# Two halves of the PE array for the decay projections: odd token tiles on rows 64 to 96, even ones on rows 0 to 32

## The reference, cut to what matters

```
k, v, lr_f, lr_b = jnp.split(p_state, STATE_SPLITS, axis=-1)
logg_f = jax.nn.log_sigmoid((lr_f @ w_dec_f + b_dec_f).astype(jnp.float32)) / GLA_TAU
logg_b = jax.nn.log_sigmoid((lr_b @ w_dec_b + b_dec_b).astype(jnp.float32)) / GLA_TAU
```

## Time and profile before

| | us |
|---|---|
| median of 3 runs | 1681.29 (1680.9 to 1683.6) |
| the profiled execution's own time | 1684.84 |
| its span, first to last instruction | 1683.0 |
| PE busy in the span | 1601.7 (95%) |
| weight loads (PEld) busy | 1353.5 (80%) |
| DVE, ACT, POOL busy | 737.2 (44%), 574.1 (34%), 605.9 (36%) |
| mean granted clock of PE | 0.981 of full |

### The profile page before, as it was taken

The page is one execution under the profiler, slowest core; times in us unless marked ns, Lnnn a source line. Parts: engine busy times, 40 slices in busy tenths (PEclk is TensorE's granted clock), DMA queues, the critical chain, the costliest instruction groups (busy, mean ns, idle before and its releaser), DMA issues.

```text
span 1683.0 us, 23322 instructions
## 1 busy us (share of the span) xinstructions
PE 1601.7 (95%) x9320; PEld 1353.5 (80%) x9320; DVE 737.2 (44%) x1207; ACT 574.1 (34%) x924; POOL 605.9 (36%) x317
## 2 busy tenths in 40 slices
PE   5999999999899999999999899999989999999997
PEld 2777887877689989998999567888886888888887
DVE  2610225836565515662366384035755321221137
ACT  3634212523643313441143155442533422222231
POOL 1422111225333623563255343332242443444441
PEclk9899999989999999999999899999999999999999
DMA  9443332135412212212222572121062222222221
GB/s 372 156 159 136 108 130 89 39 128 187 186 63 76 78 48 76 76 63 66 72 76 94 228 260 83 63 76 51 26 238 101 77 98 100 90 98 100 88 90 60
DMA packets 50210, 185.25 MB, mean 110 GB/s; under 512 B 5254, under 2 KB 10246, under 8 KB 43208
## 3 DMA queue, kind: packets, MB, share of 16 engines
q1 hardware_dynamic: 44028, 170.29, 28.6%
q10 hardware_dynamic: 6092, 13.70, 2.2%
HBM read 172.44 MB, written 11.53 MB: 109 GB/s over the span
## 4 chain that ended last, share of the span: by engine, by line
PE 82%; DVE 6%; issue 4%; ACT 3%; POOL 2%; DMA 1%; SPq 1%; ACTq 0%; DVEq 0%; POOLq 0%
PE A L975 57%; PE A L1221 7%; PE N L1221 4%; PE G L1221 4%; POOL w_lo L913 2%; PE G L1277 1%; DMA raw<-modw 1%; PE N L995 1%; PE G L995 1%; PE A L1117 1%; PE G L1083 1%; PE A L1155 1%; PE A L1149 1%; PE G L1051 1%; PE N L1067 1%
## 5 line engine op out<-in xcount | busy, mean ns | idle before, releaser
L913 POOL TENSOR_TENSOR w_lo<-raw,w_hi 128x1024 fp32r<-128x1024 f32 (+2 forms) x175 | 404.3, 2313 | 726.0 <-ACT w_hi L1304 726.0
L975 PE MATMUL A<-h_hi,w_hi 128*128 128x512 f32 (+1 forms) x1264 | 418.3, 362 | 28.3 <-DVE h_lo L2073 12.9
L975 PE MATMUL A<-h_hi,w_lo 128*128 128x512 f32 (+1 forms) x1264 | 408.5, 354 | 0.0
L975 PE MATMUL A<-h_lo,w_hi 128*128 128x512 f32 (+1 forms) x1264 | 407.9, 353 | 0.0
L1304 ACT ACTIVATE w_hi<-raw 128x1024 fp32r<-128x1024 f32 (+2 forms) x175 | 177.3, 1015 | 425.3 <-PE A L975 389.8
L975 PEld LDWEIGHTS A<-h_hi,w_hi 128*128 128x128 f32 x1264 | 224.9, 191 | 85.8 <-issue 24.6
L975 PEld LDWEIGHTS A<-h_hi,w_lo 128*128 128x128 f32 x1264 | 225.4, 192 | 33.0
L975 PEld LDWEIGHTS A<-h_lo,w_hi 128*128 128x128 f32 x1264 | 225.3, 192 | 32.0 <-issue 0.2
L975 PE MATMUL A<-g_hi,w_hi 128*128 128x512 f32 (+1 forms) x528 | 165.6, 353 | 3.8 <-DVE g_lo L1773 2.0
L975 PE MATMUL A<-g_hi,w_lo 128*128 128x512 f32 (+1 forms) x528 | 163.7, 349 | 0.0
L975 PE MATMUL A<-g_lo,w_hi 128*128 128x512 f32 (+1 forms) x528 | 163.6, 349 | 0.0
(11 more groups left out here) (294 smaller groups left out, 2509.0 us busy)
## 6 DMA issues: line engine op xcount, KB each, us to landing
raw<-stream SPq DMA_DIRECT2D x150, 512.0 KB, 3.2
mraw<-modw SPq DMA_DIRECT2D x38, 1024.0 KB, 5.4
raw<-pairs SPq DMA_DIRECT2D x18, 512.0 KB, 4.6
raw<-stream SPq DMA_DIRECT2D x24, 384.0 KB, 3.0
raw<-modw SPq DMA_DIRECT2D x6, 1024.0 KB, 14.7
x<-x_keep ACTq DMA_DIRECT2D x4, 1536.0 KB, 9.2
mraw<-pairs SPq DMA_DIRECT2D x9, 512.0 KB, 3.2
x_keep<-x SPq DMA_DIRECT2D x4, 768.0 KB, 21.5
```

Of the source, the lines that this page charges most:

```text
L913: pool.tensor_tensor(lo, like_chunk(n, raw[:, n % RAW, 0:WIDTH[n]]), hi.bitcast(F32), ALU.subtract).then_inc(lo_done, 1)
L975: m = pe.matmul(dst[:, t0:t1], a, b[:, k, t0:t1], start=(first and p == 0), stop=(last and p == 2))
```

## The change

Half of the decay projections move to other partitions.

- `lrT` and `wd` grow from 33 to 97 partitions. In both, partitions 64 to 96 play for odd token tiles what 0 to 32 are for even ones. `wd[64:97]` is a copy of `wd[0:33]`, made on the host, so that each load of `wd` brings 97 rows.
- In the weight chunk of the `lr` projection the host repeats the 32 `lr` columns as columns 64 to 95. So the accumulator of `proj` 0 has the same 32 rows again on partitions 64 to 95. The matmuls keep their shapes, since they always made 128 rows.
- ACT's one copy of 32 x 768 becomes two of 32 x 3 x 128: partitions 0 to 31 for tiles 0, 2, 4, and partitions 64 to 95 for tiles 1, 3, 5.
- DVE sets two rows of ones, 32 and 96, where it set one; `lr_ones` is counted after the second.
- The decay projection of tile `tt` takes rows 0 to 32 or 64 to 96 of `lrT` and `wd`, by `tt % 2`.

```diff
-        wd = sb("wd", [33, 512])
+        wd = sb("wd", [97, 512])
...
-                lrT = sb("lrT", [33, TOK], stack=early)
+                lrT = sb("lrT", [97, TOK], stack=early)
...
-                    pe.matmul(unit_of(e), lrT[0:33, tt * P:(tt + 1) * P], wd[:, :],
+                    rows = slice(64 * (tt % 2), 64 * (tt % 2) + 33)
+                    pe.matmul(unit_of(e), lrT[rows, tt * P:(tt + 1) * P], wd[rows, :],
                               start=True, stop=True).then_inc(full["z"], 1)
...
+                    if name == "lr":
+                        half = lambda t, r: t[64 * r:64 * r + 32, 0:T].rearrange("p (a c t) -> p c a t", c=2, t=P)[:, r, :, :]
+                        act.activation(half(lrT, 0), half(src, 0), ACT.Copy)
+                        act.activation(half(lrT, 1), half(src, 1), ACT.Copy).then_inc(free[f"A{PLAN.acc[e]}"], 1)
+                        high(n0 + RING)
+                        act.preload_act_table_set(LN_SET)
+                        continue
...
-                        dve.memset(lrT[32:33, :], 1.0).then_inc(lr_ones, 1)
+                        dve.memset(lrT[32:33, :], 1.0)
+                        dve.memset(lrT[96:97, :], 1.0).then_inc(lr_ones, 1)
...
+            if c[0] == "in" and c[2] == C_LR:
+                both = dst.reshape(P, KT, P)
+                both[:, :, 64:64 + 2 * RANK] = both[:, :, 0:2 * RANK]
...
-    wdec = _np.zeros((33, DEPTH, 512), _np.float32)
+    wdec = _np.zeros((97, DEPTH, 512), _np.float32)
...
+    wdec[64:97] = wdec[0:33]
```

More of the change, by code:

```diff
@@ L1418, in _ @@
                     act.wait_ge(chunk_used, n0 + 1)
-                    dst = {"lr": lrT[0:32, 0:T], "k": kT[:, j % 2, 0:T], "v": (vst if j < 2 else cgz)[:, j % 2, 0:T], "q": qT[:, j % 2, 0:T],
+                    if name == "lr":
[5 more added lines that the diff above has]
+                        continue
+                    dst = {"k": kT[:, j % 2, 0:T], "v": (vst if j < 2 else cgz)[:, j % 2, 0:T], "q": qT[:, j % 2, 0:T],
                            "f": uF[:, j % 2, 0:T], "c": cgz[:, j % 2, 0:T], "b": bg[:, j % 2, 0:T], "r": r_s[:, j, 0:T]}[name]
-                    rows = 32 if name == "lr" else P
                     if name == "r":
-                        m = act.activation(dst, src[0:rows, 0:T], ACT.Silu)
+                        m = act.activation(dst, src[:, 0:T], ACT.Silu)
                     else:
-                        m = act.activation(dst, src[0:rows, 0:T], ACT.Copy, scale=DK ** -0.5 if name == "q" else 1.0)
+                        m = act.activation(dst, src[:, 0:T], ACT.Copy, scale=DK ** -0.5 if name == "q" else 1.0)
                     m.then_inc(free[f"A{PLAN.acc[e]}"], 1)
@@ L1428, in _ @@
                         high(n0 + RING)
-                    if name == "lr" or (name, j) == ("r", 3):
+                    if (name, j) == ("r", 3):
                         act.preload_act_table_set(LN_SET)
```

## The result

The changed kernel takes 1686.66 us (median of 20 runs, 1681.93 to 1691.55), the kernel before 1682.51 us (median of 20 runs, 1680.06 to 1684.78). The ratio is 1.0026 with a 95% interval of 1.0018 to 1.0033: slower by 4.2 us, where a gain of 5.0 us and a time of 1676.3 us (1674.4 to 1679.8) were predicted. The median of three runs from which that time was worked out, 1681.29 us, lies 1.2 us under the median of 20; the gain is the fairer comparison.

What follows compares the result with a forecast made beforehand. PE was taken as the bound, busy 95% of the span and 82% of the chain. -5.16 us on PE and +0.2 for the late signal, say 5.0, took 1681.3 to 1676.3 us (range 1674.4 to 1679.8).

Steps and rivals of the forecast that it cites:

- PE, the two halves: Six pairs of decay projections (pieces of PE's chain): two 0.43 us slots for four, 0.86 us less each, 5.16 in all.
- The score rows: Score matmuls alternating between row halves, 0.069 us a pass against 0.124 at full height, taken as evidence that halves overlap.
- strict order: Rival: odd tile's first pass waits for even tile's second; three slots, 2.6 us gained in all, 1678.7 us; chance 0.10.
- DMA: the step that failed: Layer 1's `wd` load, 66 to 194 KB: 1 us more at the same rate, landed by 1026 us, nothing charged.
- The cover of 2.3 us: Layer 1: distance from `wd` landing by 1026 us to PE's queue asking for it at 1028.3 us.
- my rivals: Decay pairs: strict order (chance 0.10), layer 0's saving lost later (0.05), no overlap (0.04), slower (0.03).
- the one for "slower": Rival: changing rows mid-piece empties the array, 0.25 us a piece, 1.5 in all, 1683.0 us with late signal; chance 0.03.
- DVE: Layer 1's first pair: the second 0.70 us memset signals late, losing about 0.2 us of that piece's 0.86.
- ACT: Copies to `lrT`: two of about 0.52 us for one of 0.80, 0.24 us more; `kT` may come 0.05 us later.
- The layer 0 side: Layer 0: memset hidden, copies cost nothing, `wd` issued some 25 us before use; its three pieces gain 2.6 us.
- The sign that I gave for it: Layer 1 pieces should start 2.6 us earlier than before; otherwise layer 0's saving is lost later.

Runs made afterwards that it cites:

- the 98-row kernel: Changed kernel with one more row in `wd`, zeros that nothing reads, so 98 rows are loaded instead of 97: 1677.48 us, ratio to the kernel before 0.9970.
- its twin on one half: The 98-row kernel with all tiles on rows 0 to 32 again, its two copies, two memsets and longer load kept: 1683.24 us.
- the early load of 97 rows: Changed kernel with layer 1's `wd` load issued some 650 us earlier, at the start of layer 0's output projection: 1679.95 us.
- 128 rows: Changed kernel with `wd` of 128 rows in place of 97: 1679.82 us, ratio to the kernel before 0.9982.
- two loads: Changed kernel with two `wd` loads of 33 rows, to partitions 0 and 64, in place of one of 97: 1678.43 us.
- the kernel before with 97 rows: Kernel before with `wd` grown to 97 rows, its matmuls still using the first 33: 1696.20 us, ratio 1.0080.

## Why the prediction was wrong, point by point

**PE, the two halves.** Right. Two slots in place of four, 1.91 - 1.06 = 0.85 us a piece against 0.86 predicted, six times, and it reaches the end: the 98-row kernel is 5.2 us under the one before and 5.8 under its twin on one half. The score rows were the right neighbour. In strict order the pieces would have been some 1.5 us long. The changed kernel's first pair has two passes at its very start (line 1052's instructions, 66.93 to 66.96 us):

```profile
L1052 PE MATMUL G<-wd,lrT x2: 693/693/693, 66.9 to 66.9; 33*128 33x512 f32 x2
```

The even tile's two passes use the same rows and can't start together, so one of the two is the odd tile's.

**DMA: the step that failed.** "Three times the bytes at the same rate are 1 us more", and so "nothing is charged". The rate is not the same. It comes from the number of engines, and that from the number of rows. With one engine, beside the weight chunks, 97 rows took 12.70 us, where some 2.5 us were forecast (issued at 1023.48, landed by 1026). The cover of 2.3 us that I named was real, but the load took not 1 us more: it took 11 more. The rows that I had read held the sign: 44 packets in the view behind the earlier trace rows, 33 of them rows and 11 small. I read only their rate. None of my rivals had this, and the one for "slower" looked for the loss inside the array.

**The price of the wait.** 7.01 us idle and 3.0 us at the lower clock behind it. 1677.5 (the 98-row kernel) + 10.0 - 0.8 (the wait for the memset that is hidden here) gives 1686.7 us; measured 1686.66. That the two agree so closely is partly luck, since the 10.0 us come from one execution and medians here move by a microsecond or two.

**DVE: right place, and the size holds in one kernel of four.** The second memset makes the first pair of layer 1 late, as predicted. With the early load of 97 rows PE has no idle time before that pair, which takes 1.32 in place of 1.06 us: 0.26 us lost, against 0.2 forecast. In the kernels with 98 rows, 128 rows and two loads, PE also waits 0.50 to 0.52 us for the memset, 0.76 us in all for the 98-row one. Two things that the forecast took as fixed moved there. The second memset stands 0.20 us behind the first (1020.80 to 1021.00), where I had no gap; that gap is in every kernel with two long memsets. And the two small `coef` operations ahead took 0.81 us in place of 0.36. Here are POOL and DVE of the 98-row kernel:

```profile
1017.07 2.56 POOL L913 TENSOR_TENSOR w_lo<-raw,w_hi 128x1024 fp32r<-128x1024 f32 x1
1018.92 0.81 DVE L1689 SCALAR_TENSOR_TENSOR coef<-modT,par 128x8 f32<-128x8 f32 x2
```

The `coef` pair ends 0.10 us behind the end of POOL's pass (1019.73 and 1019.63). It does so in the other traces as well, 0.09 to 0.12 us behind, in the kernel before at 1027.08 and 1026.97. In the 98-row kernel it began 1.85 us into that pass, in the kernel before 2.32 us into it. So its length looks like the rest of POOL's pass; no run changes that alone. In the changed kernel itself the wait for the load covers all of this.

**ACT.** Right. Two copies of 0.48 us each against 0.52 estimated, nothing waits for them.

**The layer 0 side** came out as forecast: the load of 97 rows was issued at 42.2 us, some 25 us ahead of its first use at 67.0, nobody waited for it, and the three pieces there gave their whole gain. The sign that I gave for it, that the layer 1 pieces start 2.6 us earlier, was worthless: the kernel before with 97 rows, which gains nothing in layer 0, reached line 1011, just ahead of them, at 1023.22 us where the kernel before did at 1025.79.

## What to carry to other kernels

Two fp32 matmuls, one behind the other, ran side by side here when their operands lay on different halves of the partitions, even with satisfied waits between them: 33 rows and 512 columns in the pairs, 64 rows and 128 columns in the scores. Both wrote different PSUM banks; whether they have to was not tried. When a tile grows, look at the number of its rows as a load deals them out: 98 rows had moved 2 us after the issue and 128 landed in 2.5, where 97 took 12.7. In a trace, count the closing packets of a load (those under 512 bytes) before taking its rate for a larger one, and hold the landing time against the first use wherever a load is issued just ahead of it.

## What the runs showed of the hardware that I had not expected

- The engines that share a load: 11 for 33 rows, 1 for 97, 14 for 98, 16 for 128. One engine with nothing else to move carries a row of 2048 bytes about every 0.08 us, 25 GB/s.
- Waits of 7.0 and 7.3 us left behind them a stretch at the lower clock that cost another 3.0 and 4.4 us. Here an idle gap cost about one and a half times its length.
- The odd tile's first pass started before the even tile's second, though the odd tile's matmul stands behind the even one's in the program. In these pairs order was kept on each half of the rows by itself.
